# Last attention of a fused transformer kernel: scores two pairs ahead, standing between a pair's transposes and its values; transposes over three PSUM banks

## The reference, cut to what matters

```python
s_ctx = jnp.einsum('bqkgd,bjkd->bkgqj', qb, k_ctx).astype(jnp.float32) * scale
p = sink_softmax(jnp.concatenate([s_ctx, s_win], axis=-1), sink_b)
vals = jnp.concatenate([v_ctx, vb], axis=1)
return jnp.einsum('bkgqj,bjkd->bqkgd', p.astype(v.dtype), vals)
```

## Time and profile before

| | us |
|---|---|
| median of 3 runs | 1405.42 |
| lowest, highest | 1403.09, 1407.39 |
| profiled execution, its own time | 1403.28 |
| its span, first to last instruction | 1401.5 |
| last attention within the span | 1298.04 to 1360.73 |
| mean granted TensorE clock | 0.974 of full |

### The profile page before, as it was taken

The page is one execution under the profiler, slowest core; times in us unless marked ns, Lnnn a source line. Parts: engine busy times, 40 slices in busy tenths (PEclk is TensorE's granted clock), DMA queues, the critical chain, the costliest instruction groups (busy, mean ns, idle before and its releaser), DMA issues. The chain is left out here.

```text
span 1401.5 us, 19445 instructions
## 1 busy us (share of the span) xinstructions
PE 1299.5 (93%) x7522; PEld 758.8 (54%) x7522; DVE 457.0 (33%) x1260; ACT 322.8 (23%) x651; POOL 20.0 (1%) x34
## 2 busy tenths in 40 slices
PE   5999998997999999999999999978999889898787
PEld 2886665686544444444444444437444634487456
DVE  2117485325533333333333333333000121302752
ACT  2222323204122222222222222222100101211651
POOL 0001010000000000000000000000000000000000
PEclk8899999998999999999999999999999999899999
DMA  9856599734599999999999999930222002030000
GB/s 390 300 169 252 199 365 409 290 149 170 211 389 393 389 385 378 389 390 391 389 391 372 390 390 390 390 141 31 90 64 86 30 30 90 30 121 0 1 1 30
DMA packets 47805, 331.70 MB, mean 237 GB/s; under 512 B 5233, under 2 KB 7377, under 8 KB 7825
## 3 DMA queue, kind: packets, MB, share of 16 engines
q1 hardware_dynamic: 44640, 325.08, 58.8%
q10 hardware_dynamic: 2896, 4.24, 0.9%
q0 software_dynamic: 224, 1.77, 0.3%
HBM read 330.02 MB, written 1.05 MB: 236 GB/s over the span
## 5 line engine op out<-in xcount | busy, mean ns | idle before, releaser
L361 PE MATMUL bank<-hT,ring 128*128 128x256 f32 (+1 forms) x1024 | 295.6, 450 | 14.1 <-ACT hT L935 9.7
L361 PEld LDWEIGHTS bank<-hT,ring 128*128 128x128 f32 x1024 | 199.2, 195 | 109.2 <-issue 87.1
L652 PE MATMUL bank<-ring,arena 128*64 128x512 f32 x1088 | 240.7, 594 | 0.3 <-DMA ring<-experts 0.3
L652 PEld LDWEIGHTS bank<-ring,arena 128*64 128x64 f32 x1088 | 76.0, 137 | 136.0 <-issue 136.0
L676 PE MATMUL bank<-ring,arena 128*64 128x512 f32 x544 | 124.2, 598 | 0.0
L624 PEld LDWEIGHTS bank<-arena 128*128 128x128 bf16 x1680 | 95.3, 98 | 28.3 <-issue 28.3
L624 PE MATMUL bank<-arena 128*128 128x128 bf16 x1680 | 105.4, 219 | 0.2 <-DVE arena L1484 0.2
L632 PE MATMUL bank<-arena 128*128 128x512 bf16 x408 | 95.3, 384 | 4.6 <-DVE arena L1520 4.6
L1059 ACT COPY arena<-bank 128x512 f32<-128x512 f32 x70 | 41.0, 585 | 172.5 <-PE bank L624 172.5
L1516 DVE TENSOR_TENSOR arena<-bank,arena 128x512 f32<-128x512 f32 x68 | 43.8, 686 | 105.0 <-ACT arena L1068 105.0
L676 PEld LDWEIGHTS bank<-ring,arena 128*64 128x64 f32 x544 | 36.0, 136 | 61.8 <-issue 58.2
(11 more groups left out here) (284 smaller groups left out, 1214.1 us busy)
## 6 DMA issues: line engine op xcount, KB each, us to landing
ring<-experts SPq DMA_DIRECT2D x204, 1024.0 KB, 7.5
ring<-stream SPq DMA_DIRECT2D x105, 1024.0 KB, 6.9
arena<-consts POOLq DMA_DIRECT2D x1, 1472.0 KB, 7.5
resid<-x SPq DMA_DIRECT2D x1, 1024.0 KB, 5.9
resid<-ctx ACTq DMA_DIRECT2D x1, 1024.0 KB, 5.3
out<-arena ACTq DMA_DIRECT2D x8, 128.0 KB, 2.1
arena<-rpb ACTq DMA_DIRECT2D x2, 438.0 KB, 22.4
cs<-consts ACTq DMA_DIRECT2D x1, 480.5 KB, 9.3
```

What stands on the lines that cost most here:

```text
L361: mm = mmul(o[:, 0:n_tok], w[:, k, t * P:(t + 1) * P], hT[:, k, 0:n_tok], start=(k == 0), stop=(k == KT - 1))
L652: mm = mmul(bank[B_GU][64 * u:64 * u + 64, :], xg[:, kk, SLOTS * u:SLOTS * u + SLOTS], w[u][:, k, :], start=(kk == 0), stop=(kk == KT - 1))
```

## The change

On TensorE, for the last attention alone, scores(0) and scores(1) come ahead of the loop, and the loop is turn(2i), turn(2i+1), scores(i+2) if there is such a pair, values(i). The transposes' groups rotate over banks 2, 3 and 5, and all values go to bank 4. On ScalarE the exponents of pairs 0 and 1 come first, then for each i the copies of pair i and the exponents of pair i+2. On VectorE c_scores of heads 0 to 3 come first, and within the loop c_scores(2i+4) and (2i+5) stand where (2i+2) and (2i+3) stood. c_out(i-1) stays last in the loop. The two other attentions keep their order and banks.

```diff
                     for j in range(per):
                         name = (kind, "t", h, j)
-                        o = open_group(name, 2 + (h % 2 if per == 1 else j))
+                        o = open_group(name, 2 + h % 2 if per == 1 else (2, 3, 5)[(2 * h + j) % 3])
...
                     name = (kind, "o", i)
-                    o = open_group(name, 4 + i % 2)
+                    o = open_group(name, 4 + i % 2 if per == 1 else 4)
...
                 scores(0)
+                if kind == "c":
+                    scores(1)
+                    for i in range(n_heads // 2):
+                        turn(2 * i)
+                        turn(2 * i + 1)
+                        if 2 * i + 4 < n_heads:
+                            scores(i + 2)
+                        values(i)
+                    return
...
+                if kind == "c":
+                    exponents(0)
+                    exponents(1)
+                    for i in range(8):
+                        turned(i)
+                        if i < 6:
+                            exponents(i + 2)
+                    return
...
-            c_scores(0)
-            c_scores(1)
+            for h in range(4):
+                c_scores(h)
             for i in range(8):
                 for h in (2 * i, 2 * i + 1):
                     dve.wait_ge(S("c_exp"), h + 1)
                     a = att[:, h % 4, :]
                     link(v.tensor_tensor(a[:, 4:6], a[:, 4:6], a[:, 6:8], ALU.add))
                     normalise("c", h, 512)
-                if i < 7:
-                    c_scores(2 * i + 2)
-                    c_scores(2 * i + 3)
+                if i < 6:
+                    c_scores(2 * i + 4)
+                    c_scores(2 * i + 5)
                 if i >= 1:
                     c_out(i - 1)
             c_out(7)
```

More of the change, by code:

```diff
@@ L434, in attention @@
                         scores(i + 1)
-                    if kind in ("na", "mla") and i == 0:
+                    if i == 0:
                         ada_fold(1 if kind == "na" else 2)
@@ L999, in attention, with exponents @@
                 n_heads, _, nk = KINDS[kind]
-                for i in range(n_heads // 2):
+                def exponents(i):
                     for h in (2 * i, 2 * i + 1):
@@ L1016, in attention, with turned @@
                             ins.then_inc(S(kind + "_exp"), 1)
-                    if kind in ("na", "mla") and i == 3:
-                        ada_quarters(2 if kind == "na" else 3)
+                def turned(i):
                     for h in (2 * i, 2 * i + 1):
@@ L1022, in attention @@
                             emptied(a.copy(pT[:, h % 2, 512 * j:512 * j + 512], bk((kind, "t", h, j))[:, :]), (kind, "t", h, j))
+                if kind == "c":
[6 more added lines that the diff above has]
+                    return
+                for i in range(4):
+                    exponents(i)
+                    if i == 3:
+                        ada_quarters(2 if kind == "na" else 3)
+                    turned(i)
             attention("na")
```

## The result

The changed kernel takes 1424.73 us (median of 4 runs, 1423.82 to 1426.91), the kernel before 1405.62 (4 runs beside it): ratio 1.0141, 95% interval 1.0125 to 1.0158. The change costs 19 us. The forecast was 1425. The profiled execution has 1423.82 us, 20.54 more than the profiled one of before.

What follows compares the result with a forecast made beforehand. In the last attention nothing is saturated, so order and waits decide, along TensorE and ScalarE. Profiled 1403.28 us plus 10.2 at full clock gave 1413.5, plus 10.5 for clock falls 1424.0; stated as 1425, range 1411.5 to 1434.

Steps and rivals of the forecast that it cites:

- The ring and its length: Last attention: values, transposes, scores, evictions and c_out wait on each other in turn; period 8.77 us against 7.10.
- Idle time before the values: Last attention: TensorE idle from the end of scores to c_out, 3.0 us in each of five periods.
- VectorE's wait for scores: Last attention: VectorE waits for scores some 2 us a pair, where it waited for none.
- The second ring: Scores, evictions, c_out, normalise twice, last transposes, scores: 8.43 us by itself, so a second values bank would hardly help.
- Full-clock sum: Last attention's head, four middle periods and tail at full clock: +10.2 us, from 1403.28 to 1413.5.
- The clock: Waits near 3 us in the last attention drop TensorE's clock: seven slow stretches at 1.5 us, 10.5; chance 0.65.
- The clock that holds: Rival: TensorE's clock doesn't fall after the last attention's waits, so the time is 1413.5 us; chance 0.17.
- The clock that stays low: Rival: a fall lasts more than one stretch, twelve instead of seven, giving 1431.5 us; chance 0.14.
- a gain: Rival: TensorE's own work sets the last attention's period, 5.95 us, giving 1395.2; chance 0.02.
- The edits granted: Last attention: moved scores cover TensorE's 0.82 us wait, the third transpose bank its 0.33; 1.15 a period.

Runs made afterwards that it cites:

- e8: Kernel before with the new banks (three for transposes, one for values) and c_out(i-1) moved ahead of the period's two c_scores: 1401.70 us, 0.9981.
- e5: Kernel before with the changed kernel's order on TensorE alone; VectorE, ScalarE and banks as before: 1403.96 us, 0.9989.
- e6: Changed kernel with scores(i+2) ahead of the transposes, values one pair late, c_out(i-2) ahead of the evictions, two pT buffers, old banks: 1400.22 us, 0.9965.
- e9: The kernel with values one pair late (e6), but with transposes over three banks and all values on one: 1399.38 us, 0.9960.
- e1: Changed kernel's order on all three engines with the old banks, transposes on two and values alternating over two: 1424.38 us, 1.0151.
- e2: Kernel before, its order kept, with the new banks alone (transposes over three, all values on bank 4): 1407.59 us, 1.0023.
- e3: Changed kernel with c_out(i-1) moved ahead of the two c_scores in VectorE's loop: 1420.41 us, 1.0116.
- e4b: Changed kernel with TensorE's idle time filled by matmuls whose result is overwritten (the filled kernel): 1416.63 us, 1.0078.

## Why the prediction was right

- *The ring and its length.* Forecast 8.77 us, measured 8.83 at full clock (8.82 in the filled kernel). Two of its terms were off, by +0.33 and -0.24, and their all but cancelling is luck: the first eviction comes 1.30 us after the scores start (I took 0.97, half of the time at half clock), and from there to c_out it is 1335.93 - 1332.67 = 3.26 (I had 0.36 + 3.14 = 3.50). The first tile comes later, so the third matmul holds up the second tile (at 1333.39, 0.72 behind the first instead of 0.61) by 0.11 only.
- *Idle time before the values.* Forecast 3.0, measured 3.04, five times, put down to c_out's line, L1679 now. VectorE's wait for scores was forecast at some 2 a pair and is 2.78.
- *The second ring.* I said that a second bank for the values would change the period little, to 8.43. With the old banks no time comes back (1424.4 against 1424.7), but every period there has a fall of the clock, so 8.43 itself was never seen; c_out first, which takes the same wait away and shortens the second ring too, gives 8.09.
- *Full-clock sum.* Forecast +10.2; the kernel with filled idle time has a stage 10.5 us longer than before, in the three parts that were forecast: +7.5 until values(1) (forecast 7.4), +6.9 in four periods (6.7), -3.9 behind values(5) (-3.8).
- *The clock.* Forecast seven stretches at 1.5 us, 10.5. There are six slow places behind the first scores (the transposes of pairs 0 and 1, and values 2 to 5), 8.8 us by the filled kernel, 1.47 each. The size of one fall was right, their number one too large: of the five waits of 3.04, the one before 1327.57 passed without a fall, while the one of 2.02 in the head had its own. That 1424.0 lies 0.2 from the profiled 1423.8 is luck: 1.7 us too many here are made up by 1.2 that this execution was late before the stage and 0.3 in the full-clock sum. Two rows that this term and the ring used are not wholly at half clock: the granted clock is 0.56 over the 1.94 us from 1298.04, and 0.62 over the transposes from 334.43.
- *Rivals.* The clock that holds (1413.5) is what the filled kernel shows and not what the changed kernel does: its stage is 10.5 us longer than before, as that sum has it, and its median is 1416.6 since, in its profile at least, 3.2 us more lie ahead of the stage. The Trainium skill's advice that I had put against the term (page "TensorE: Matmul & The Clock Gate", section "Why this matters for your kernels") is to keep gaps between bursts of matmuls below some 3 us. By that advice the gaps here were at the edge; the traces do not bear it out as a safe bound: after four of five waits of 3.04 the clock was down, and most waits of 2.02 and all five of 2.35 were followed by falls too. The clock that stays low did not come about, nor a gain.
- *The edits granted.* The third bank and the covered copies do what they are for: the waits for ScalarE are gone in the middle of the stage. They were worth up to 1.15 us a pair. Without the ring, e8 (the banks) and e5 (the scores over the copies) are 3.3 and 1.7 us below the kernel before, e5 not clear of noise; e6 and e9, which cover the copies by late values, are 5.5 and 5.6 below it.

One reading of mine failed, in an expectation and not in the prediction: that c_out(i-1) ends well before values(i) in the old order. I had taken c_out at 1323.85 for the next pair's.

## What to carry to other kernels

When a producer's work is moved behind something that its consumer must release first, look at the consumer's queue: if it takes the product in the same round in which it releases the producer, the two engines work in turns; a second bank for the values didn't change that here. Go round such a ring once, add up the durations, and compare with the busiest engine's own work; here 8.8 against 6.0. Then count the idle time that TensorE gets per round, because here a wait of 2 to 3 us cost itself and, mostly, another 1.5 us of slow matmuls behind it.

## What the runs showed of the hardware that I had not expected

- Work that is thrown away can make a kernel faster: about 2.7 us of fillers a period, granted clock 1.00 instead of 0.87 in the stage, 8.1 us less.
- A wait of the same length doesn't always bring a fall: of five waits of 3.04 us one passed, and in the run with c_out first two of six of 2.02. Behind the first scores of the stage, over the changed kernel, e1, e2 and e3, 19 of 22 waits of 2.02 to 3.24 us were followed by a fall; the waits of 1.12 to 1.87 in the stages of e2, e4b, e6 and e9 were not. Even unchanged code goes both ways: ahead of the stage, the wait of 1.70 before L397 passed in the profile of the kernel before, and in the changed kernel's the clock fell behind it. The two windows below are the kernel before and the changed one; from these scores to the next values, the records of L427 at 241.05 and 244.09, it is 7.32 and 10.47 us. What decides that these runs don't show.

```profile
233.62 0.67 PE L397 MATMUL bank<-arena 96*128 96x256 f32 x2 [1.70 <-ACT pr L1020]
```

```profile
233.60:241.60 8.00, 6.90 (x74) 4.77 (x76) 3.36 (x12) 2.67 (x9) 0.00 (x0) 1.00 0.99 394
233.60:241.60 8.00, 7.83 (x52) 5.00 (x56) 3.32 (x12) 0.79 (x4) 0.00 (x0) 0.57 0.67 258
```

- VectorE gets its first tile of scores 1.30 us after the scores' start at full clock, and 1.94 in the head of the stage before, at a granted clock of 0.56. At a delay that follows the clock, 1.30 would become 2.3, an estimate from these two numbers; so part of it seems not to.
